# Two of the first loads are issued by ScalarE's DMA queue instead of SyncE's

## The reference

```python
h = jnp.concatenate([meta, x, ...], axis=1)          # 272 x 1024
a = rmsnorm(h, norm_mix_pre[0])                      # h * rsqrt(mean(h*h)) * gain
a = a @ w_dqkv                                       # q latent: 384 columns, kv latent: 256, rope: 32
c_q = rmsnorm(c_q, q_norm)
```

## Time and profile before

| | before |
|---|---|
| median of 3 runs | 898.21 us (897.73 to 898.43) |
| span of the profiled execution | 896.4 us |
| TensorE busy | 882.7 us, 98% of the span |
| VectorE, ScalarE, GpSimd busy | 75%, 56%, 18% |
| granted TensorE clock, mean | 0.998 |
| DMA | 146.81 MB, 164 GB/s over the span |

### The profile page before, as it was taken

The page is one execution under the profiler, slowest core; times in us unless marked ns, Lnnn a source line. Parts: engine busy times, 40 slices in busy tenths (PEclk is TensorE's granted clock), DMA queues, the critical chain, the costliest instruction groups (busy, mean ns, idle before and its releaser), DMA issues.

```text
span 896.4 us, 19632 instructions
## 1 busy us (share of the span) xinstructions
PE 882.7 (98%) x7222; PEld 857.7 (96%) x7222; DVE 675.9 (75%) x1167; ACT 503.2 (56%) x853; POOL 163.6 (18%) x158
## 2 busy tenths in 40 slices
PE   9999999999999999999999999999999999999997
PEld 8977889999999998899999999999999999999997
DVE  7768459999994446999999544889888788875556
ACT  6777665666665347766666535554455444444443
POOL 0029530000001004200000003200032333313312
PEclk9999999999999999999999999999999999999999
DMA  7652134545455631354456454344434555564441
GB/s 251 197 126 88 58 132 158 177 181 187 167 213 184 236 152 47 107 189 182 180 187 223 168 204 158 118 166 141 141 142 171 196 188 185 186 229 176 170 141 48
DMA packets 25778, 146.81 MB, mean 164 GB/s; under 512 B 3040, under 2 KB 9216, under 8 KB 10496
## 3 DMA queue, kind: packets, MB, share of 16 engines
q1 hardware_dynamic: 25584, 145.99, 46.0%
q10 hardware_dynamic: 144, 0.13, 0.0%
HBM read 142.84 MB, written 1.05 MB: 161 GB/s over the span
## 4 chain that ended last, share of the span: by engine, by line
PE 94%; DVE 3%; ACT 1%; DMA 1%; issue 1%; POOL 0%; SPq 0%; DVEq 0%; POOLq 0%
PE bank L519 27%; PE bank L520 26%; PE bank L521 26%; PE bank L868 2%; PE bank L1091 1%; PE bank L884 1%; PE bank L657 1%; PE bank L672 1%; PE bank L902 1%; PE bank L640 1%; PE bank L812 1%; DMA k_heads<-w_dq_dram 1%; PE bank L1048 1%; PE bank L557 1%; PE bank L551 1%
## 5 line engine op out<-in xcount | busy, mean ns | idle before, releaser
L519 PE MATMUL bank<-u_high,w_high 128*128 128x256 f32 (+2 forms) x1318 | 376.6, 286 | 2.7 <-ACT u_high L1254 1.2
L520 PE MATMUL bank<-u_low,w_high 128*128 128x256 f32 (+2 forms) x1318 | 374.1, 284 | 0.0
L521 PE MATMUL bank<-u_high,w_low 128*128 128x256 f32 (+2 forms) x1318 | 373.0, 283 | 0.0
L519 PEld LDWEIGHTS bank<-u_high,w_high 128*128 128x128 f32 x1318 | 248.9, 189 | 5.7 <-ACT m L1226 1.7
L520 PEld LDWEIGHTS bank<-u_low,w_high 128*128 128x128 f32 x1318 | 248.6, 189 | 0.0
L521 PEld LDWEIGHTS bank<-u_high,w_low 128*128 128x128 f32 x1318 | 248.4, 188 | 0.0
L1675 DVE TENSOR_TENSOR w_low<-raw,w_high 128x1024 fp32r<-128x1024 f32 (+6 forms) x106 | 181.2, 1710 | 88.9 <-ACT w_high L1208 87.4
L1208 ACT ACTIVATE w_high<-raw 128x1024 fp32r<-128x1024 f32 (+6 forms) x115 | 179.9, 1565 | 66.8 <-PE bank L521 62.5
L519 PE MATMUL bank<-x_high,w_high 128*128 128x256 f32 (+1 forms) x592 | 167.9, 284 | 0.4 <-DVE x_low L2257 0.3
L521 PE MATMUL bank<-x_high,w_low 128*128 128x256 f32 (+1 forms) x592 | 168.2, 284 | 0.0
L520 PE MATMUL bank<-x_low,w_high 128*128 128x256 f32 (+1 forms) x592 | 167.3, 283 | 0.0
(11 more groups left out here) (290 smaller groups left out, 1140.4 us busy)
## 6 DMA issues: line engine op xcount, KB each, us to landing
raw<-w_up_dram SPq DMA_DIRECT2D x66, 1024.0 KB, 4.8
raw<-w_down_dram SPq DMA_DIRECT2D x24, 1408.0 KB, 5.9
raw<-w_gin_c_dram SPq DMA_DIRECT2D x4, 1536.0 KB, 6.7
raw<-w_wo_dram SPq DMA_DIRECT2D x4, 1024.0 KB, 5.4
raw<-w_wout_dram SPq DMA_DIRECT2D x4, 1024.0 KB, 4.7
raw<-w_pgate_dram SPq DMA_DIRECT2D x4, 1024.0 KB, 4.8
raw<-w_gin_v_dram SPq DMA_DIRECT2D x2, 1024.0 KB, 4.7
raw<-w_gin_g_dram SPq DMA_DIRECT2D x2, 1024.0 KB, 5.5
```

Source lines behind the costliest of these rows:

```text
L519: nc.tensor.matmul(out, hi, rhi, start=start, stop=False)
L520: nc.tensor.matmul(out, hi, rlo, start=False, stop=False)
L521: return nc.tensor.matmul(out, lo, rhi, start=False, stop=stop)
```

## The change

The gains and the first weights piece leave SyncE's queue and are issued by ScalarE, ahead of its table load: first the weights piece, then the gains. SyncE issues the rest in the order it had.

```diff
         @block.sync
         def _(sp):
-            sp.dma_start(par[:, 0:DC], dram["par"][:, 0:DC]).then_inc(gains_in, 16)
             for p, cols in enumerate(first_pieces()):
                 sp.dma_start(h[:, 2 * p:2 * p + 2, :], dram["h0"][:, 2 * p:2 * p + 2, :]).then_inc(h_in[p], 16)
-                sp.dma_start(first_weights[:, cols], dram["w_dq"][0, :, cols])\
-                    .then_inc(loaded[0] if p == PIECES - 1 else pieces_in[p], 16)
+                if p > 0:
+                    sp.dma_start(first_weights[:, cols], dram["w_dq"][0, :, cols])\
+                        .then_inc(loaded[0] if p == PIECES - 1 else pieces_in[p], 16)
...
+            first = first_pieces()[0]
+            act.dma_start(first_weights[:, first], dram["w_dq"][0, :, first]).then_inc(pieces_in[0], 16)
+            act.dma_start(par[:, 0:DC], dram["par"][:, 0:DC]).then_inc(gains_in, 16)
 
             act.wait_ge(*done("ones"))
```

## The result

The change made the kernel slightly slower: 899.48 us (median of 21 runs, 898.41 to 900.26) against 898.21 us for the kernel before (21 runs, 897.56 to 898.65). The ratio is 1.0015, with a 95% interval of 1.0009 to 1.0022. The forecast was 898.1 with a range up to 899.2, and slightly faster; the measured time lies above the range. The profiled execution of the changed kernel took 899.21 us at a span of 897.4 us.

A forecast was written before the change was run, and what follows sets the result against it. TensorE was taken to bound the kernel, its sums held by VectorE's first unit; h 2 0.45 us earlier and gains 0.55 later would nearly cancel, ending VectorE at 14.45 instead of 14.57, hence 898.1 us, range 897.0 to 899.2.

The forecast's parts named there:

- What bounds it: TensorE, continuous from 15.20 us; any shift of the sums' start at 14.67 reaches the kernel's end one for one.
- VectorE's chain: VectorE's first unit ends at the later of G + 9.80 and h 2's landing + 5.50; forecast 14.45 against 14.57.
- G: Time when both gains and h 0 are there, for ScalarE's and VectorE's first instruction; 4.1 before, forecast 4.65.
- ScalarE's issues and table load: Two DMA issues on ScalarE delay its table load 0.8 to 0.95 us, hidden in its 1.85 us wait for h 0.
- the bracket of 4.34 to 4.81 for weights 0: Landing of weights 0 beside h 0: 4.81 if their 4.07 us stays, 4.34 if 0.47 between issues is saved.
- The turning point: At VectorE's end: G can grow by 0.66 us, to 4.77, before the end moves; beyond that one for one.
- h 2's landing: On SyncE's queue, the last load VectorE waits for: 8.62 instead of 9.07, 0.45 us earlier.
- the faster rival: Gains not held back, G at or below 4.3: VectorE ends 0.45 to 0.74 us earlier, 897.8 to 897.5; chance 0.3.
- The rival that came true: Gains land late, holding both engines' first instruction: 0.5 to 0.81 us slower, 898.7 to 899.0; chance 0.25.

The follow-up runs named there:

- h 1 held back: Against the changed kernel, SyncE issues h 1 and all loads behind it only when the gains have landed; 899.5 us in one execution.
- gains in two: Against the changed kernel, the gains come as two transfers of half the columns, same bytes in twice the rows; 901.93 us, repeated 900.93 us (ratio 1.003).

## Why the prediction was wrong

In one table, from the profiles (us; the last column is the span less the start of the sums):

```
version                        first chunk  VectorE ends  sums start  span   rest
only gains on ScalarE             3.69         13.57        13.68     895.4  881.7
only gains on ScalarE, again      3.77         13.65        13.75     895.3  881.6
gains ahead of weights 0          3.73         13.62        13.84     895.3  881.5
gains ahead of weights 0, again   3.77         13.66        14.02     895.4  881.4
h 0, gains, weights 0 on SyncE    3.60         14.36        14.46     896.2  881.7
before                            4.09         14.57        14.67     896.4  881.7
only weights 0 on ScalarE         5.00         14.88        14.99     896.8  881.8
before, again                     4.20         15.02        15.13     896.8  881.7
the change, again                 5.77         15.65        15.75     897.3  881.6
the change                        5.78         15.67        15.77     897.4  881.6
h 1 held back                     5.07         16.02        16.12     897.7  881.6
weights 1 ahead of h 1            6.17         16.05        16.15     897.8  881.7
gains in two, again               6.94         16.82        17.56     899.1  881.5
gains in two                      6.99         16.87        18.62     900.1  881.5
```

- **What bounds it: right.** The prediction carried the start of the sums to the end one for one. The rest is 881.4 to 881.8 us in all these executions, over 4.9 us of differences.
- **VectorE's chain: right.** G + 9.80 was forecast. Where VectorE did not wait for `h`, it ended 9.88 to 9.89 us after the first chunk (5.78, 3.69, 3.73 and others), 0.08 more than the sum.
- **ScalarE's issues and table load: right.** They cost nothing; the load moved from 0.74 to 1.67, and ScalarE still waited 2.62 us afterwards.
- **G, the time at which the gains are there: mis-sized, and this is the step that failed.** It was put at 4.65: the middle of the bracket of 4.34 to 4.81 for weights 0, "with a little for the gains behind the weights", which leaves less than 0.1 us for the gains. Weights 0 landed at 4.94, 0.13 above the bracket, and the "little" measured 0.84 us. No row stood behind it. The prediction looked at the order on ScalarE's own queue and took nothing for what SyncE's queue would have in flight beside the gains; what counts there is their rows, eight turns on each engine, each as long as a row of h 1. G was 5.78, 1.13 too late (0.77 by the gains, 0.36 by weights 0), and 5.78 + 9.80 = 15.58 by the prediction's own formula; the sums started at 15.77.
- **The turning point: right**, against the first profile of before. The end moves from G = 4.77 on. G came 1.01 us above it, and the sums moved by 1.10. In the second profile of before h 2 came 0.45 us later, and the turning point with it.
- **h 2's landing: mis-sized the other way.** 8.62 was forecast, 7.2 measured. The forecast let the stream move on by 0.45 us at its old rate, but the rate was another: 407 GB/s from 5 to 7 us instead of 269, for a reason that no run separated. It cost no time, since VectorE was held by G. Together with a G of 3.7, earlier than the 4.03 that the faster rival was worked out with, it is why two of the other versions gain 0.7 to 0.9 us where the faster rival stopped at 0.45 to 0.74.
- **The rival that came true** was the late gains, with a chance of 0.25. Its place, its price of one for one and its turning point were right. Its term for G was not: it reached 5.58 at its worst by letting weights 0 share the engines with h 1, and gave the gains nothing. In fact weights 0 landed 0.2 us behind h 0 and it was the gains that shared with h 1. That 5.58 lies near the 5.78 measured is in part luck.
- **The rule of the Trainium skill** ("DMA: Bandwidth & Descriptors", section "Issuing engines are not separate DMA queues") says that DMAs from several engines interleave and only issue time is saved. The trace agrees that they interleave (73 rows against 74, above). By the rule there was nothing to lose; measured was a loss of 1.10 us at the sums, because interleaving has a price for a load of many short rows.
- **The range** ended at 899.2, the late-gains rival's 0.81 plus some scatter. It was too narrow by 0.3 us for the 21 runs; the 899.11 of the repeat lies inside it. That the time would stay within 0.2% of before was right.

## What to carry to other kernels

A small transfer that gates the first instructions of two engines should not be queued behind a large one, nor run beside one if it can be helped. In these runs it was priced well by counting its rows per DMA engine and taking each at one row of whatever the other queue was moving, and it landed about 0.2 us behind a load of as many rows beside it (in all but the version with only weights 0 on ScalarE's queue, where it came ahead). A wait with two releasers has slack on one of them; work out where the other takes over (here 4.77) before moving either. Splitting loads over two queues helped only in the two versions that had the short rows at the head of the second queue.

## What was unexpected of the hardware

- 4 KB in 128 rows took 1.7 us from issue to landing at the head of the only queue in use, 3.0 us beside one large load even when first on its queue, and 4.6 us behind one and beside another.
- Putting those 128 short rows between two large loads of one queue went with a rate of 198 and 256 GB/s in the two us around it (one profile).
- TensorE's clock fell after an idle stretch of 2.84 us (granted 0.50), and 36 rows cost 10.12 us instead of 8.49. In the first execution of the same kernel, after 2.38 us, rows of up to 792 ns tell the same, though the granted clock read 1.00 there. After 1.18 and 1.56 us (the change, and weights 1 ahead) the 36 rows took 8.49 us as ever. So the loss has a second step: gains that came 1.16 us later than in the change (6.94 against 5.78) moved the sums by 1.79 us (17.56 against 15.77).
